# An expert layer's rarely taken path moved ahead of its last two quads, the combine behind its own down calls, additions by half tile, half score levels, and mixer projections by row halves (one core)

## The reference

```python
for layer in range(2):
    hmix = rms_norm(x, mix_norm[layer])
    if layer == 0: x = x + hgrn2_mixer(hmix, ...)      # gated linear recurrence, 8 heads, w_in 1024x4096
    else:          x = x + moba_mixer(hmix, ...)       # causal attention over the shared K/V, with a bias
    x = x + hier_moe(rms_norm(x, ffn_norm[layer]), ...)
    if layer == 0: k_blocks, v_blocks, k_mean = shared_kv(x, kv_norm, w_kv, k_norm)

# hgrn2: f = lb + (1 - lb) * sigmoid(f_logit); k = 1 - f; decay by products of f
#        o_t = sum_{s<=t} (q_t * decay(s..t) . k_s) v_s ; o = rms_norm(o) * silu(g) ; o @ w_out
# hier_moe: top-1 of 4 groups, top-2 of its 8 experts; 32 experts, each
#        (silu(x @ w_in[:, :512]) * (x @ w_in[:, 512:])) @ w_out, weighted and added per token
```

## Time and profile before

| | |
|---|---|
| three runs, us | 1273.73, 1274.07, 1275.2 (median 1274.07) |
| profiled execution, us | 1273.23, span 1271.4 |
| PE busy | 894.1 us (70%), 5118 instructions |
| DVE, ACT, POOL busy | 280.1, 120.5, 19.2 us |
| mean granted PE clock | 0.856 |
| DMA | 446.62 MB, mean 351 GB/s |

### The profile page before, as it was taken

How to read it: one execution, slowest core, us unless ns; L and a number is a source line. 1 busy time by engine, 2 the same in 40 slices (tenths; PEclk the granted TensorE clock), 3 DMA queues, 4 the chain that set the end, 5 groups by cost and what they waited for, 6 DMA issues and landing times.

```text
span 1271.4 us, 12063 instructions
## 1 busy us (share of the span) xinstructions
PE 894.1 (70%) x5118; PEld 421.8 (33%) x5118; DVE 280.1 (22%) x449; ACT 120.5 (9%) x313; POOL 19.2 (2%) x23
## 2 busy tenths in 40 slices
PE   7999997755657466556479999776475656664756
PEld 6865655221213121222124455522131212222211
DVE  4358434202011020202031251420210202020202
ACT  1000011100000000010001132110000000000000
POOL 1000010000000000000000100000000000000000
PEclk9999998978778687887789999897887868888768
DMA  9793243899999999999999525389999999999995
GB/s 346 190 362 135 75 190 133 359 421 427 427 429 427 429 429 429 428 427 428 419 399 393 196 108 198 133 359 428 428 427 428 427 428 428 429 429 427 428 417 230
DMA packets 54161, 446.62 MB, mean 351 GB/s; under 512 B 4449, under 2 KB 6793, under 8 KB 29537
## 3 DMA queue, kind: packets, MB, share of 16 engines
q1 hardware_dynamic: 53136, 443.30, 84.3%
q0 software_dynamic: 976, 2.63, 1.3%
HBM read 443.28 MB, written 2.62 MB: 351 GB/s over the span
## 4 chain that ended last, share of the span: by engine, by line
DMA 47%; PE 43%; SPq 4%; DVE 3%; issue 2%; ACT 1%; DVEq 0%
PE ps L1016 42%; DMA ring<-in_moe_w_in 30%; DMA ring<-in_moe_w_out 16%; SPq L364 2%; SPq L301 2%; PE ps L1019 1%; DVE work L739 1%; DVE work L729 0%; DMA xs<-in_x 0%; DVE xs L953 0%; DVE work L648 0%; DVE work L722 0%; DVE work L724 0%; ACT work L496 0%; ACT work L486 0%
## 5 line engine op out<-in xcount | busy, mean ns | idle before, releaser
L1016 PE MATMUL ps<-ring,work 128*32 128x512 f32 (+1 forms) x3456 | 626.3, 706 | 331.0 <-DMA ring<-in_moe_w_in 241.2
L1016 PEld LDWEIGHTS ps<-ring,work 128*32 128x32 f32 (+1 forms) x3456 | 199.6, 138 | 711.0 <-issue 700.1
L1016 PE MATMUL ps<-work 128*128 128x128 f32 (+4 forms) x1090 | 191.8, 349 | 7.2 <-DVE work L729 2.2
L897 DVE TENSOR_SCALAR work<-work 128x512 f32<-128x512 f32 x16 | 6.8, 427 | 720.8 <-ACT work L544 720.8
L1016 PEld LDWEIGHTS ps<-work 128*128 128x128 f32 (+2 forms) x1090 | 136.7, 193 | 76.0 <-issue 71.5
L496 ACT ACTIVATE work<-ps,first 128x128 f32<-128x128 f32 x128 | 36.5, 368 | 298.2 <-PE ps L1016 298.2
L1016 PE MATMUL ps<-work,ring 128*128 128x256 f32 x256 | 55.8, 380 | 1.3 <-issue 1.3
L899 DVE RECIPROCAL work<-work 128x512 f32<-128x512 f32 x16 | 53.6, 3353 | 0.5
L1016 PEld LDWEIGHTS ps<-work,ring 128*128 128x128 f32 x256 | 48.5, 190 | 8.7 <-issue 2.2
L549 ACT COPY work<-ps 128x512 f32<-128x512 f32 x32 | 18.7, 585 | 333.4 <-PE ps L1016 333.4
L1019 PE MATMUL ps<-first,work 128*128 128x128 f32 x184 | 26.4, 290 | 16.1 <-DVE work L682 8.1
(11 more groups left out here) (114 smaller groups left out, 237.7 us busy)
## 6 DMA issues: line engine op xcount, KB each, us to landing
ring<-in_moe_w_in SPq DMA_DIRECT2D x120, 2048.0 KB, 20.2
ring<-in_moe_w_out SPq DMA_DIRECT2D x52, 2048.0 KB, 20.4
ring<-in_moe_w_in SPq DMA_DIRECT2D x16, 1024.0 KB, 19.5
ring<-in_moe_w_out SPq DMA_DIRECT2D x32, 512.0 KB, 15.2
ring<-in_hg_w_in SPq DMA_DIRECT2D x7, 2048.0 KB, 20.3
work<-in_moe_w_out SPq DMA_DIRECT2D x4, 2048.0 KB, 9.8
ring<-in_w_kv SPq DMA_DIRECT2D x4, 2048.0 KB, 19.6
ring<-in_hg_w_out SPq DMA_DIRECT2D x2, 2048.0 KB, 21.1
```

What stands on the lines that cost most here:

```text
L1016: return pe.matmul(o, l, r, start=start, stop=stop)
```

## The change

1. `over` is called inside `over_quads`, ahead of the last two quads, on all four engines. It now leaves its sums in the PSUM banks instead of adding to `xs`, uses other banks, and works on a shifted copy of the positions.
2. `combine` of a quad stands behind its own down calls, and signals each of its four matmul pairs; the next writers of `y` and `spread` wait for that.
3. The sums are added to `xs` in four pieces of 512 columns, each with a signal (`moe_added`); PE's transposes and the output DMAs wait for the pieces they read.
4. Score levels 1 to 7: PE writes and DVE copies only the columns of odd blocks. The order of gate and V projections is the table `VG`, and `silu_gate` comes one level later.
5. The chunks of output, K, Q and V projections are halves of the rows: `project_rows` multiplies four slices `k` of a tile by 512 columns, in two parts that add up in one bank. At the border the transposes for K are copied for both tiles ahead of the squares, and those for Q behind.

```diff
+VG = [(1, 0), (0, 0), (1, 1), (0, 1), (1, 2), (1, 3), (0, 2), (0, 3)]
-        def over_quads(eng, body):
+        def over_quads(eng, body, further_passes):
             body(0)
             with eng.Fori(1, ITERS - 1) as it:
                 body(it)
+            further_passes()
             body(ITERS - 1)
...
-            for c, j in enumerate((0, 1, 6, 7, 4, 5)):
+            for c, j in enumerate((0, 1, 6, 4, 7, 5)):
                 load(MIX0 + 2 + c, up_view(MIX0 + 2 + c), cols(hg_w_in[0], j))
             for j in range(2):
-                load(MIX0 + 8 + j, up_view(MIX0 + 8 + j), cols(hg_w_out[0], j))
+                load(MIX0 + 8 + j, rows_view(chunk(MIX0 + 8 + j)), row_half(hg_w_out[0], j))
...
-            for a in range(TT):
-                sp.wait_ge(x_ready, a + 1)
-                sp.dma_start(out[0, a * P:(a + 1) * P, :], xs[:, a, :]).then_inc(out_done, 16)
-            sp.wait_ge(out_done, 16 * TT)
+            for i in range(4):
+                a, half = i // 2, slice((i % 2) * 512, (i % 2 + 1) * 512)
+                sp.wait_ge(moe_added, 4 + i + 1)
+                sp.dma_start(out[0, a * P:(a + 1) * P, half], xs[:, a, half]).then_inc(out_done, 16)
+            sp.wait_ge(out_done, 16 * 4)
...
+            for l, (kind, i) in enumerate(VG):
+                half = slice((i // 2) * 512, (i // 2 + 1) * 512)
+                act.wait_ge(vg_done, l + 1)
+                if kind:
+                    act.activation(gate[:, i % 2, half], ps[:, 4 + l % 4, :], ACT.Exp, scale=-1.0).then_inc(g_exp, 1)
+                else:
+                    if i == 0:
+                        act.wait_ge(biasout, 16)
+                    act.copy(v_all[:, i % 2, half], ps[:, 4 + l % 4, :]).then_inc(v_ready, 1)
...
+                if l == 0:
+                    dve.copy_predicated(sdiag, masks[:, 0:1, :].to_broadcast([P, 2 * H, P]), scored).then_inc(pred_done, 1)
+                else:
+                    def odd(v):
+                        return v.rearrange("p b (n two m) -> p b n two m", two=2, m=m)[:, :, :, 1, :]
+
+                    dve.copy_predicated(odd(sdiag), odd(masks[:, l:l + 1, :]).to_broadcast([P, 2 * H, P // (2 * m), m]),
+                                        odd(scored)).then_inc(pred_done, 1)
...
             for l in range(LEVELS + 1):
                 level(l)
-                if l < 4:
-                    silu_gate(l)
+                if l and VG[l - 1][0]:
+                    silu_gate(VG[l - 1][1])
...
-                over_quads(dve, body)
-                dve.wait_ge(nblk_ready, layer + 1)
-                n = dve.value_load(nblk[0:1, layer:layer + 1], min_val=1, max_val=MAXPASS)
-                for a in range(TT):
-                    dve.wait_ge(c_done, 2 * (P0 + QUADS) - 1 + a)
-                    link(dve.tensor_tensor(xs[:, a, :], xs[:, a, :],
-                                           ps[:, 2 * a:2 * a + 2, :].rearrange("p b n -> p (b n)"), ALU.add))
-                over(layer, n)
+                over_quads(dve, body, lambda: over(layer))
+                for i in range(4):
+                    dve.wait_ge(c_done, 4 * (P0 + QUADS) - 3 + i)
+                    dst = xs[:, i // 2, (i % 2) * 512:(i % 2 + 1) * 512]
+                    dve.tensor_tensor(dst, dst, ps[:, i, :], ALU.add).then_inc(moe_added, 1)
...
+            def project_rows(c, j, lhs, bank, a, half):
+
+                arrived(c)
+                for k in range(KD // 2):
+                    i = mm(ps[:, bank, :], lhs[:, j * (KD // 2) + k, a * P:(a + 1) * P],
+                           rows_view(chunk(c))[:, k, half * 512:(half + 1) * 512],
+                           j == 0 and k == 0, j == 1 and k == KD // 2 - 1)
+                return i
...
+                def asked(v):
+                    return v if l == 0 else v.rearrange("p (n two m) -> p n two m", two=2, m=1 << (l - 1))[:, :, 1, :]
...
+                        i = mm(asked(ps[:, b // 4, (b % 4) * P:(b % 4 + 1) * P]), k3[:, h, a * P:(a + 1) * P],
+                               asked(q3[:, h, a * P:(a + 1) * P]))
...
+                    for j in range(2):
+                        pe.wait_ge(oT_ready, 6 + 2 * j if layer else 2 * a + j + 1)
+                        for half in range(2):
+                            i = project_rows(c + j, j, lhs, 4 + 2 * a + half, a, half)
+                            if j:
+                                i.then_inc(pr_done, 1)
...
-                        if not (is_int(it, 0) and u == 0):
-                            combine(it, u - 1, is_int(it, 0) and u == 1, False)
...
-                over_quads(pe, body)
-                combine(ITERS - 1, UN - 1, False, True)
-                over(layer)
+                        combine(it, u, is_int(it, 0) and u == 0, last)
+
+                over_quads(pe, body, lambda: over(layer))
...
             for a in range(TT):
-                pe.wait_ge(xn_ready, 4 + a + 1)
-                transposes(4 + a, a, 4 + 2 * a, xs)
+                transposes(4 + a, a, 4 + 2 * a, xs, lambda half: pe.wait_ge(moe_added, 2 * a + half + 1))
+            for a in range(TT):
+                hT_ready(5 + a)
+                for half in range(2):
+                    project_rows(MIX1, 0, hkvT, 2 * a + half, a, half)
...
+            def att_v(part):
+                j, half = part // 2, part % 2
+                if j == 0:
+                    pe.wait_ge(kqT_ready, 2 * half + 2)
```

More of the change, by code:

```diff
@@ L1008, in _ @@
             moe(1)
-            for a in range(TT):
-                dve.memset(mark[:, a:a + 1], 0.0).then_inc(x_ready, 1)
         @block.tensor
@@ L1022, in arrived, with transposes @@
                 pe.wait_ge(loaded[c % RING], it * (16 * TURNS) + 16 * (c // RING + 1))
-            def transposes(n, a, bank, src):
+            def transposes(n, a, bank, src, half_in=lambda half: None):
                 for k in range(KD):
+                    if k % 4 == 0:
+                        half_in(k // 4)
                     i = tr(ps[:, bank + k // 4, (k % 4) * P:(k % 4 + 1) * P], src[:, a, k * P:(k + 1) * P])
@@ L1099, in out_and_router @@
             def out_and_router(layer, n, c, lhs):
-                for i in range(4):
-                    a, half = i // 2, i % 2
-                    if layer == 0 and half == 0:
+                for a in range(TT):
+                    if layer == 0:
                         if a:
@@ L1228, in gather_for @@
                     gather(None, 5, 1, gat_done)
[L1230 removed]
+                pe.wait_ge(xn_ready, (4, 6)[layer])
                 gather_for(0, 0)
```

167 lines of the change are left out of this document (82 added, 85 removed).

## The result

| | before | after |
|---|---|---|
| median, us (four runs each) | 1274.41 (1273.73 to 1275.2) | 1260.95 (1258.69 to 1261.29) |
| ratio, 95% interval | | 0.9888 (0.9875 to 0.99) |
| profiled execution, us; span | 1273.23; 1271.4 | 1260.97; 1259.1 |
| mean granted PE clock | 0.856 | 0.848 |

A forecast was written before the change was run, and what follows sets the result against it. Transfers bound the expert stages, PE's order of work the rest. Terms 2.2 + 1.2 + 1.1 + 6.5 + 0.7 - 0.7 + 2.3 = 13.3 us, taken from 1274.07, gave 1260.8 us; range 1257 to 1267.

The forecast's parts named there:

- The rule of the sum: Whole kernel: mixer gains move the end in full; PE work moved inside expert stages counts nothing unless releases exceed slack.
- The border: Between the layers: check gone, quarter adds, transposes at full clock; K's projection 5.5 us earlier, faster projections 1.0, together 6.5.
- Rival B: Border between layers: PE at half clock or another wait hidden there; 4.0 us or less gained, 1263.3 to 1267 us; 17%.
- The price of the check: Check moved before the last two quads: 4.3 us, fitting with combine and y's copy (8.6) into PE's 9.96 us idle.
- the second cover: Expert stages: a late slot release at 624.45 stays hidden while the queue is busy until 635.6, 11 us.
- Gate before the next level: Score levels: new projection order and silu one level later remove PE's two waits for DVE, 1.61 and 0.56; gain 2.2 us.
- Half score levels on PE: Score levels 1 to 7: 64 columns instead of 128, 0.106 us an instruction instead of 0.112; gain 1.2 us.
- Rival A: Score levels: time goes with columns, so 64-column matmuls take half; 12.5 us gained instead of 1.2, 1249.5 us; 5%.
- rival D: Expert stages: combine and check ahead of the up calls delay a release, 4.3 us a layer, 1269.4 us; 4%.
- Rival C: Score levels 1 to 6: spaced columns slow on PE, up to 1282 us; 5% for over the whole gain, 5% for part.
- Output projections and V: Row halves: first output projection gains 1.1 us, second 0.7; V's first half waits for another copy, losing 0.7.
- The end: Kernel's end: shorter last add 0.5, no DVE branch 0.7, one fewer issue 0.7, half the last bytes 0.6; 2.3 us taken.

The follow-up runs named there:

- e6: Changed kernel with the check for further passes made twice in a row ahead of the last two quads; median 1259.14 us, ratio to before 0.9883.
- e12: Changed kernel with the old order of gate and V projections and silu, and all 128 score columns on PE; half copies stay; 1260.7 us.
- e8: Changed kernel with each 512-column Q projection matmul split into two of 256 columns, read and written at a step of 2 elements; 1258.54 us.
- e1: Changed kernel with the check for further passes behind the last quad again on all four engines; median 1268.73 us, ratio to before 0.995.
- e3: Changed kernel with PE writing all 128 columns of a level's scores, DVE still copying only the odd ones; 1260.47 us.
- e5: Changed kernel with the score levels as before: old order, silu place and chunk order, 128 columns on PE, whole copies on DVE; 1262.26 us.
- e4: Changed kernel with the old order of gate and V projections, silu and chunks; half columns and half copies stay; 1264.2 us.

## Why the prediction was right, and where it was not

- **The rule of the sum** (mixer gains count in full, work moved inside an expert stage for nothing) held: the expert stages changed by 0.2 and 0.1 us, and with twice the check (e6) they didn't grow. It is not as strict as the prediction had it: e12 and e8 gave 2.1 and 1.6 us of a longer mixer stage back in the two stages behind it.
- **The border**, 6.5 forecast, 6.46 measured (5.61 and 0.85), for the reason given. What the prediction had left as "issue, with its own check in it" is the branch alone (e1), and the slow clock of transposes and first projections went with it. Rival B, 17%, did not occur; the first weights were there in time.
- **The price of the check** was wrong: 4.3 us, read from PE's idle at the old place, was only the part that stuck out. The branch takes 6.0 to 6.5 us (up to 7.1 in e6) and began under the combine. Added up as the prediction did, that makes 3.7 + 0.6 + 6.3 = 10.6 us in a gap of 9.96. Nothing was late, because the branch begins at 545.6, under a combine that ends at 547.4; and had it been late, the second cover would have held (e6).
- **Gate before the next level**, 2.2 forecast from two brackets, 2.9 measured for the stage. From start to start PE's levels 1 to 4 took 12.21, 10.70, 11.23 and 10.57 us in before, and 10.44 each in after. The brackets hold 1.61 and 0.56; of the other 0.8, 0.3 is that a bracket counts from the end of a group (7.03 us long, 6.87 from start to start), and levels 3 and 5 start 0.15 and 0.14 us behind the end of DVE's copy, in waits too small for a bracket. The term should have been read from starts, not brackets. Nor does the account given, 10.6 us of DVE against 10.5 of PE, make a pause of 1.61. At level 1 DVE began 0.9 us behind the start of PE's scores and worked 11.1 us, from 81.50 to 92.63; with 0.15 to PE's next start that is the 12.2.
- **Half score levels on PE**, 1.2 forecast, 0.0 (e3). The step that failed took the router's 0.106 us at 36 columns for 64 columns; they took 0.110 (3.52/32). And the 0.05 us that PE gains on a level's scores it gives back on the projection behind them. The two errors in the levels offset each other: 3.4 forecast, 2.9 measured.
- **The halved copy**, "2.43 to about 1.2 us, seven times", was right at five levels and wrong at levels 1 and 2. It was costed at nothing, so it moved no number. In the old order it is worth 0.9 us with full columns (e12 against e5), and the new order another 2.1 (e3 against e12); the new order with whole copies was not run. With half columns as well, the old order is worse than before (e4).
- **Rival A** (columns count, 5%) and **rival D** fell. **Rival C** fell for this change, since at every level at least two of the four elements in 16 bytes are wanted; its mechanism exists at a step of 4, and then at the price named for it (0.227 in place of 0.112; 0.217 had been taken as its end).
- **Output projections and V**: 1.1, 0.7 and -0.7 forecast; 0.8, 0.8 and -0.6 measured.
- **The end**, 2.3 forecast, 3.6 measured: a mis-sized term. Of the issues 1.4 us were to go (with DVE's branch), and 1.9 went: before's two issues took 0.35 and 1.04 us, not 0.7 each, one takes 0.33 to 0.35 us here, and the first three are out while DVE still adds. What was called DVE's branch, 0.69 us, was the branch for 0.06 us only, and what else held DVE there is open; the time from the last issue to the end of the span fell by 1.1 where I had 0.6.

Misses of +0.7 (gate), -1.2 (half columns), +1.3 (end) and -0.3 (output projection) nearly cancelled, and of the 14.1 us that the stages give the medians show 13.5, with the start of the first projection between them. The mechanisms were right in the main; the agreement to 0.2 us is luck.

## What to carry to other kernels

A check that skips code which is rarely run can cost PE 3 to 7 us each time; look for it by its source line, and put it where PE waits for weights anyway, ahead of work with slack rather than behind the last matmul. Measure a stage from start to start: brackets show only the waits that are large, and a group's length can shrink while the next one grows by as much. Halving 128 columns bought nothing here, where PE's weight loads filled the time of the scores (3.65 of 3.65 us in the window of before above); take it only if another engine gains, and then look at the size of the groups that engine copies (here four elements or more).

## What the runs showed of the hardware

- A branch on PE that skips a long body took 6.0 to 7.1 us beside full transfers and 3.3 to 4.0 us at the kernel's end, and ended 1.3 to 1.5 us behind a packet of 0.02 MB on the instruction queue. PE's branch back in a loop took 0.08 to 0.24 us.
- A float32 matmul read at a step of 16 bytes took 0.227 us for 128 columns, dense 0.112; at a step of 8 bytes 256 columns took 0.227, dense 0.217. An output at a step of 8 bytes cost at most 0.01 us with it; at 16 bytes it cost nothing beyond the reading.
- DVE's copy by mask took 2.43 us for 1024 elements in groups of one or two, and 1.24 to 1.29 in groups of four and more, against 2.43 for 2048 dense.
- With scores of 64 columns and a pause of 1.61 us the granted clock was 0.63 and then 0.83 (one trace); with 128 columns and the same pause it was 1.00 (three traces).
